# Decay rows of a Mamba-2 mixer picked from transposed cumulated sums by identity columns, and the causal mask moved to VectorE

## The chip, the cores and the metric

The kernel runs on one core of a Trainium2 chip. The metric is the device time of one execution in microseconds (us), as the median of several runs. Below, TensorE is PE in the profile's rows (its weight loads are PEld), VectorE is DVE, ScalarE is ACT, GpSimd is POOL, and SP is the engine that issues the DMAs.

## The reference

Two layers, each a mixer stage and a stage of experts, on 256 tokens of width 1024. The mixer has three groups of heads side by side: windowed attention (6 heads), a bidirectional Mamba-2 (6 heads, 2 chunks of 128 tokens), and differential attention (4 heads). What the change touches is the decay matrix of the Mamba-2 heads:

```python
da = jnp.cumsum((dt * a).reshape(b, nc, SSD_CHUNK, h), axis=2)
lower = jnp.tril(jnp.ones((SSD_CHUNK, SSD_CHUNK), dtype=bool))[None, None, :, :, None]
seg = da[:, :, :, None, :] - da[:, :, None, :, :]
decay = jnp.exp(jnp.where(lower, seg, -jnp.inf))
y_diag = jnp.einsum('bclsh,bcshp->bclhp', jnp.einsum('bclhn,bcshn->bclsh', ch, bh) * decay, xdt)
...
y = y_fwd + y_bwd + d_skip[:, None] * xs
```

For each of 6 heads and 2 directions an exponential is taken of (cumulated sum of the column's token minus that of the row's token), with a mask, and multiplied by the products of C and B.

## The kernel before

**The order.** All engines walk one list, `ORDER`, of named steps (`sc.3`, `row.2.1`); each engine executes those of its own set (`ON_PE`, `ON_DVE`, `ON_ACT`) strictly in the list's order and counts its finished steps in one semaphore. A step on two engines is done by TensorE first, then ScalarE, then VectorE. The list holds for each of the two layers; after it come the 32 experts of the layer, which TensorE works through while SP streams their weights through a ring of 8 slots of 2 MB, each refilled when the step that last reads it is done.

**Steps around the change.** `cum` multiplies `dta` (dt times a, tokens on partitions) by triangles of ones, so that the cumulated sums of all heads lie as columns, tokens on partitions. `cb` makes the C-B products, `xdt` the scaled inputs. `sc.u` are attention scores (TensorE), mask, bias and maximum (VectorE), exponential (ScalarE); `nm.h` normalises them (VectorE); `pT`, `oa`, `od` turn and use them. `vz`, `ck`, `cv` are projections.

**The decay of head h, direction d (`row.h.d`).** TensorE spreads one column of `dta` over 128 columns and multiplies it by a triangle (L583), which gives the cumulated sums as a row that is the same on all partitions; this for three blocks of 128 tokens. For two of them it adds the mask by a bf16 product of `identb` and `smask` (L586). So a step is 3 f32 and 2 bf16 matmuls. ScalarE takes three exponentials from PSUM with the negated column of `cum` as bias into `E[d]` (L834 to L836). VectorE multiplies `E[d]` by the C-B products (L1093 to L1097). `y.h` then does six matmuls with both `E` (L594). There is one `E` for each direction, so the exponentials of head h wait for `y.(h-1)`.

**Banks.** PSUM has 8 banks of 512 f32. A step's bank is given out in turn; `HELD` names the step whose reader must be done before a bank is written again.

Of the kernel before, what the change touches and what calls it, by code (L numbers as in the profile page):

```python
# [132 lines left out]
PE_STEPS = list(COUNT["pe"])  # L133
FIRST_OUT = PE_STEPS.index(("outA", 0))
BANK, HELD = {}, {}
_last, _n = {}, 0
for _i, _s in enumerate(PE_STEPS):
    if _s[0] == "seed":
        continue
    if _s[0] in ("outA", "outB"):  # L140
        BANK[_s] = _s[1]
    elif _s[0] == "ov":
        BANK[_s] = 7
    else:
        BANK[_s] = _n % 8 if _i < FIRST_OUT else 4 + _n % 4
        _n += 1
    if BANK[_s] in _last and _s[0] != "outB":
        HELD[_s] = _last[BANK[_s]]
    _last[BANK[_s]] = _s
# [8 lines left out]
def build_encoder(nc, x_in, cols, rows, w_in, w_out, w_router, w_gate, w_up, w_down, final_w, out):
    with ExitStack() as ctx:
# [583 lines left out]
        def _(act):  # L743
# [16 lines left out]
            for li in range(DEPTH):  # L760
# [3 lines left out]
                for s in STEPS:  # L764
# [58 lines left out]
                    elif kind == "zs":  # L823
                        act.wait_ge(done["dve"], nth(li, "dve", ("silu", 4))) if s[1] == 0 else act.wait_ge(done["dve"], nth(li, "dve", ("zs", 0)))
                        last = A(tmp[:, :], vz[:, s[1], A_K:], ACT.Tanh, scale=0.5)
                    elif kind == "row":
# [1 line left out]
                        c = d * S_H + h
                        act.wait_ge(done["dve"], nth(li, "dve", ("cum",)))
                        if h == 0 and d == 0:  # L830
                            act.wait_ge(done["pe"], nth(li, "pe", ("xs", 1)))
# [503 lines left out]
```

## Time and profile before

| what | value |
|---|---|
| median of 3 runs | 1340.1 us (1339.53 to 1346.42) |
| profiled execution | 1351.05 us, of which 1349.3 us span |
| TensorE busy | 1016.5 us (75%) |
| VectorE busy | 382.1 us (28%) |
| ScalarE busy | 191.6 us (14%) |
| mixer stage of layer 0, of layer 1 | about 12 to 192 us, about 692 to 870 us of the span |

How to read it: a row of the timeline is start, duration, engine, source line, operation, output<-inputs, shapes, and how many records were merged (an f32 matmul leaves two records); in brackets stands how long the engine sat idle before it and what released it. PE's busy time is an upper measure, since its ends are modelled.

### The profile page before, as it was taken

The numbers are of one execution on the slowest core, as the hardware profiler recorded it, in microseconds if no ns is written. First come the engines' busy times: TensorE is split into PE (matmuls) and PEld (weight loads), VectorE is DVE, ScalarE is ACT, GpSimd is POOL, SyncE is SP. The second block draws the span as 40 slices with busy tenths as digits, with TensorE's granted clock in tenths as the row PEclk, the third lists the DMA queues.
The fourth block names the chain that finished last, engine by engine and source line by source line (L and its number), as shares of the span: only waits on it lengthen the run. The fifth ranks groups of instructions, "written<-read, shape, count | busy, mean of one in ns | idle before, by whom it ended". The sixth has DMA issues, their size and how long they took to land.

```text
span 1349.3 us, 26710 instructions
## 1 busy us (share of the span) xinstructions
PE 1016.5 (75%) x11124; PEld 639.6 (47%) x11124; DVE 382.1 (28%) x1160; ACT 191.6 (14%) x549; POOL 9.1 (1%) x28
## 2 busy tenths in 40 slices
PE   5999977766667887767679999766775767766864
PEld 5877753333334443334358777534432433333432
DVE  4456451211212222111144465512111111111112
ACT  2144210000000111000021443100000000000001
POOL 2000000000000000000000000000000000000000
PEclk9899989878888999977979999779877888888887
DMA  9822129999999989799993220289999999999992
GB/s 324 343 93 84 45 88 367 425 424 424 426 426 424 404 335 426 310 403 414 411 377 125 74 115 33 94 347 425 424 425 425 425 424 424 424 426 426 424 419 115
DMA packets 46015, 437.50 MB, mean 324 GB/s; under 512 B 8064, under 2 KB 10112, under 8 KB 21248
## 3 DMA queue, kind: packets, MB, share of 16 engines
q1 hardware_dynamic: 45824, 434.72, 78.1%
q8 instruction: 149, 2.44, 0.7%
q14 instruction: 42, 0.34, 0.1%
HBM read 433.65 MB, written 1.05 MB: 322 GB/s over the span
## 4 chain that ended last, share of the span: by engine, by line
PE 58%; DMA 22%; issue 13%; DVE 5%; ACT 1%; DVEq 1%; ACTq 0%
DMA ring<-in_w_up 22%; PE ps L465 20%; PE ps L537 7%; PE ps L476 7%; PE ps L485 4%; PE ps L446 4%; PE ps L654 4%; PE ps L549 2%; PE ps L609 2%; PE ps L583 1%; PE ps L594 1%; PE ps L553 1%; PE ps L453 1%; PE ps L616 1%; PE ps L633 1%
## 5 line engine op out<-in xcount | busy, mean ns | idle before, releaser
L465 PE MATMUL ps<-ring,xg 128*32 128x256 f32 x4096 | 337.7, 487 | 240.6 <-issue 173.3
L465 PEld LDWEIGHTS ps<-ring,xg 128*32 128x32 f32 x4096 | 173.2, 138 | 386.5 <-issue 348.7
L943 DVE SCALAR_TENSOR_TENSOR gu<-th,ps 128x128 f32<-128x128 f32 x72 | 20.7, 287 | 704.1 <-ACT th L750 704.1
L476 PE MATMUL ps<-ring,actT 128*32 128x256 f32 x2304 | 139.2, 382 | 15.2 <-issue 12.9
L750 ACT ACTIVATE th<-ps 128x128 f32<-128x128 f32 x72 | 20.0, 277 | 609.5 <-PE ps L465 609.5
L476 PEld LDWEIGHTS ps<-ring,actT 128*32 128x32 f32 x2304 | 69.0, 109 | 76.3 <-issue 20.5
L537 PE MATMUL ps<-hT,ring 128*128 128x256 f32 x416 | 97.6, 395 | 1.3 <-DVE hT L993 1.3
L537 PEld LDWEIGHTS ps<-hT,ring 128*128 128x128 f32 x416 | 81.4, 199 | 13.5 <-ACT aneg L788 2.1
L446 PE MATMUL ps<-xh,Pb 128*32 128x256 f32 x1024 | 81.1, 400 | 2.4 <-issue 2.4
L485 PE MATMUL ps<-ysb,PwT 32*128 32x256 f32 x1024 | 75.5, 404 | 2.5 <-issue 1.5
L485 PEld LDWEIGHTS ps<-ysb,PwT 32*128 32x128 f32 x1024 | 47.3, 186 | 32.5 <-issue 29.0
L654 PE MATMUL ps<-ring,hT 128*128 128x256 f32 x256 | 59.1, 389 | 2.9 <-ACT hT L858 1.6
L754 ACT ACTIVATE ysb<-ps 128x256 f32<-128x256 f32 x64 | 24.5, 383 | 234.7 <-PE ps L476 234.7
L654 PEld LDWEIGHTS ps<-ring,hT 128*128 128x128 f32 x256 | 49.0, 195 | 10.4 <-ACT hT L858 2.0
L446 PEld LDWEIGHTS ps<-xh,Pb 128*32 128x32 f32 x1024 | 39.5, 116 | 28.5 <-issue 9.2
L465 PE MATMUL ps<-ring,xgx 128*32 128x256 f32 x512 | 34.4, 428 | 12.2 <-DMA ring<-in_w_up 8.0
L842 ACT ACTIVATE pbuf<-pbuf,nmx 128x256 f32<-128x256 f32 x56 | 28.0, 500 | 58.8 <-DVE nmx L1123 25.4
L953 DVE STREAM_TRANSPOSE xraw<-ps 128x256 f32<-128x256 f32 x72 | 30.0, 417 | 16.8 <-PE ps L446 16.8
L947 DVE STREAM_TRANSPOSE actT<-actv 128x128 f32<-128x128 f32 x72 | 29.3, 407 | 5.8 <-issue 0.5
L465 PEld LDWEIGHTS ps<-ring,xgx 128*32 128x32 f32 x512 | 18.3, 123 | 26.3 <-issue 13.2
L935 DVE TENSOR_TENSOR Pw<-Pb,W 128x256 f32<-128x256 f32 x64 | 27.2, 425 | 6.6 <-issue 0.8
L955 DVE TENSOR_TENSOR xg<-xraw,fnw 128x256 f32<-128x256 f32 x64 | 27.2, 426 | 5.1 <-issue 0.4
(249 smaller groups left out, 831.5 us busy)
## 6 DMA issues: line engine op xcount, KB each, us to landing
ring<-in_w_gate SPq DMA_DIRECT2D x64, 2048.0 KB, 23.7
ring<-in_w_up SPq DMA_DIRECT2D x64, 2048.0 KB, 25.1
ring<-in_w_down SPq DMA_DIRECT2D x64, 2048.0 KB, 19.3
ring<-in_w_in SPq DMA_DIRECT2D x8, 2048.0 KB, 19.2
ring<-in_w_out SPq DMA_DIRECT2D x4, 2048.0 KB, 19.7
ring<-in_w_in SPq DMA_DIRECT2D x2, 1584.0 KB, 14.6
x<-in_x SPq DMA_DIRECT2D x1, 1024.0 KB, 5.1
out<-fin SPq DMA_DIRECT2D x2, 512.0 KB, 2.7
```

What stands on the lines that cost most here:

```text
L446: last = mm(b_prep[j * SLOTS:(j + 1) * SLOTS, 0:DQ], picks[:, t, :], xh[:, t, j * DQ:(j + 1) * DQ], start=(t == 0), stop=(t == TT - 1))
L465: last = mm(b_gate[j * SLOTS:(j + 1) * SLOTS, 0:2 * GQ], tokens[:, k, :], ring[:, low:high + 1:high - low, o:o + GQ], start=(k == 0), stop ...
L476: last = mm(b_y[j * SLOTS:(j + 1) * SLOTS, 0:DQ], actT[:, c * SLOTS:(c + 1) * SLOTS], ring[:, slot, o:o + DQ], start=(c == 0), stop=(c == ...
L485: last = mm(ps[j][:, t * DQ:(t + 1) * DQ], places_[r, t, :], y[r, :], start=False, stop=False, skip_group_check=True)
L537: last = mm(bank[:, 0:SEQ], lhs, hT[:, k, :], start=(k == 0), stop=(k == KC - 1))
L549: last = mm(bank[:, :], hT[:, k, t * P:(t + 1) * P], w[:, k, :], start=(k == 0), stop=(k == KC - 1))
L654: last = mm(bank[:, t * DQ:(t + 1) * DQ], mixT[:, c, t * P:(t + 1) * P], w_half[c // OUT_ROWS][:, c % OUT_ROWS, j * DQ:(j + 1) * DQ], star ...
L842: last = A(pb[:, t, :], pb[:, t, :], ACT.Exp, bias=nmx[:, 1, u, t:t + 1], scale=A_SCALE if u < A_H else C_SCALE, accum_out=den[:, u, t:t + 1])
L935: return v.tensor_tensor(weighted[:, :, :].rearrange("p t (j s) -> p t j s", j=NQ), picks[:, :, :].unsqueeze(2).broadcast_to(four), W[:, : ...
L947: v.transpose(actT[:, :].rearrange("p (c s) -> p c s", c=FC), actv[:, :].rearrange("p (q c) -> p c q", c=FC)).then_inc(S["actT_ready"], 1)
L953: v.transpose(xraw[:, :, :], b_prep[:, 0:DQ].rearrange("p (q k) -> p k q", k=KC))
L955: v.tensor_tensor(to[:, :, :], xraw[:, :, :], fnw[:, :].unsqueeze(2).broadcast_to([P, KC, SLOTS]), ALU.mult).then_inc(S["xg_ready"], 1)
```

## The change

`row` loses its matmuls. In their place:

- `cumT` (once a layer, right after `cum`): 4 matmuls with `dta` as the stationary operand give the cumulated sums transposed, heads on partitions (44 wide: the 12 columns stand twice, at partition 0 and at 32), for 2 directions by 256 tokens. ScalarE copies them to SBUF (`cumT`, in the memory of `yc`).
- `rows.i` (3 a layer, one for heads 2i and 2i+1): 4 matmuls of 12 partitions and 256 columns; the stationary operand is one column of the identity, spread over 128 columns, and picks one row of `cumT` onto all partitions. Direction 0 works from partitions 0 to 11, direction 1 from 32 to 43; each direction has a bank of its own.
- `seg.h.d` (12 a layer, VectorE): two operations of 128x128 add the negated column of `cum` to the row in PSUM and take the minimum with `smask`, which now holds a huge positive number or a huge negative one, into `E[d]`. It waits for `y.(h-1)`, as ScalarE did.
- ScalarE's part of `row` is one exponential of 128x128 from PSUM and one of 128x256 in place in `E[d]`, instead of three.
- The list is changed: `y.0` stands ahead of head 1's decay, `sc.2` ahead of head 2's, `y.4` ahead of `ck.0` and of head 5's.
- Banks are given out by who will be read first, and one step may be held by two.
- `dta` is widened to 44 columns, zeroed in `par` and written by two operations; `identb` goes, `smask` becomes f32.

```diff
-    conv.3 xbc.4 dt silu.2 conv.4 cq.0 xs.0 cq.1 aq.0 silu.3 dta aq.1 xs.1 lam silu.4 aq.2 cum ak cb.0 xdt cb.1 sc.0
-    nm.0 row.0.0 row.0.1 sc.1 vz.0 nm.1 row.1.0 y.0 pT.0 row.1.1 row.2.0 row.2.1 sc.2 y.1 row.3.0 row.3.1 zs.0 sc.3
-    pT.1 y.2 nm.2 vz.1 nm.3 y.3 row.4.0 row.4.1 sc.4 row.5.0 zs.1 row.5.1 ck.0 y.4 ck.1 nm.4 sc.5 pT.2 y.5 pT.3 sc.6
+    conv.3 xbc.4 dt silu.2 conv.4 cq.0 xs.0 cq.1 aq.0 silu.3 dta aq.1 xs.1 lam silu.4 aq.2 cum cumT ak cb.0 xdt cb.1 sc.0
+    nm.0 rows.0 seg.0.0 seg.0.1 row.0.0 row.0.1 sc.1 vz.0 nm.1 y.0 pT.0 seg.1.0 seg.1.1 row.1.0 row.1.1 rows.1 sc.2 y.1 seg.2.0 seg.2.1 row.2.0 row.2.1 seg.3.0 seg.3.1 row.3.0 row.3.1 zs.0 sc.3
+    pT.1 y.2 nm.2 vz.1 nm.3 y.3 rows.2 seg.4.0 seg.4.1 row.4.0 row.4.1 sc.4 y.4 zs.1 seg.5.0 seg.5.1 row.5.0 row.5.1 ck.0 ck.1 nm.4 sc.5 pT.2 y.5 pT.3 sc.6
...
+            _b = min(range(0 if _i < FIRST_OUT else 4, 8), key=lambda k: (read_at(_held_by[k]) if k in _held_by else -1, k))
...
-                    elif kind == "row":
-
-                        _, h, d = s
-                        tri = (upto, since)[d]
-                        c = d * S_H + h
-                        pe.wait_ge(done["dve"], nth(li, "dve", ("cum",)))
-                        for o, t, masked in ((0, 0, True), (1, 1 - d, False), (2, 1, True)):
-                            last = mm(bank[:, o * P:(o + 1) * P], dta[:, t, c:c + 1].broadcast_to([P, P]), tri[:, :],
-                                      start=True, stop=not masked)
-                            if masked:
-                                last = mm(bank[:, o * P:(o + 1) * P], identb[:, :], smask[:, d, :], start=False, stop=True)
+                    elif kind == "cumT":
+
+                        for d, tri in enumerate((upto, since)):
+                            for t in range(TT):
+                                last = mm(bank[0:ROWS, d * SEQ + t * P:d * SEQ + (t + 1) * P], dta[:, t, :], tri[:, :],
+                                          start=True, stop=True)
+                    elif kind == "rows":
+
+                        if s[1] == 0:
+                            pe.wait_ge(done["act"], nth(li, "act", ("cumT",)))
+                        for a in range(2):
+                            for d in range(2):
+                                r = slice(32 * d, 32 * d + 2 * S_H)
+                                c = 32 * d + d * S_H + 2 * s[1] + a
+                                last = mm(ps[BANK["row", 2 * s[1] + 1, d]][:, a * SEQ:(a + 1) * SEQ],
+                                          ident[r, c:c + 1].broadcast_to([2 * S_H, P]), cumT[r, d, :], start=True, stop=True)
...
-                        if h > 0:
-                            act.wait_ge(done["pe"], nth(li, "pe", ("y", h - 1)))
-                        A(E[d][:, 0, :], bank[:, 0:P], ACT.Exp, bias=cum[:, 0, 0, c:c + 1])
-                        A(E[d][:, 1, :], bank[:, P:2 * P], ACT.Exp, bias=cum[:, d, 2, c:c + 1])
-                        last = A(E[d][:, 2, :], bank[:, 2 * P:3 * P], ACT.Exp, bias=cum[:, 1, 0, c:c + 1])
+                        act.wait_ge(done["dve"], nth(li, "dve", ("seg", h, d)))
+                        seg_rows, off = ps[BANK["row", h | 1, d]], h % 2 * SEQ + (1 - d) * P
+                        A(E[d][:, 1, :], seg_rows[:, off:off + P], ACT.Exp, bias=cum[:, d, 2, d * S_H + h:d * S_H + h + 1])
+                        last = A(E[d][:, 0:3:2, :], E[d][:, 0:3:2, :], ACT.Exp)
...
+                    elif kind == "seg":
+
+                        _, h, d = s
+                        dve.wait_ge(done["pe"], nth(li, "pe", ("rows", h // 2)))
+                        if (h, d) == (0, 0):
+                            dve.wait_ge(done["pe"], nth(li, "pe", ("xs", 1), ("cb", 1)))
+                        if h > 0:
+                            dve.wait_ge(done["pe"], nth(li, "pe", ("y", h - 1)))
+                        seg_rows, c = ps[BANK["row", h | 1, d]], d * S_H + h
+                        for t in range(TT):
+                            o = h % 2 * SEQ + t * P
+                            last = v.scalar_tensor_tensor(E[d][:, 2 * t, :], seg_rows[:, o:o + P], cum[:, t, 0, c:c + 1],
+                                                          smask[:, d, :], ALU.add, ALU.min)
```

## Rows read from the trace of the kernel before

**Rows 1.** The page: busy share of the DMA engines in 40 slices, in tenths

```profile
DMA  9822129999999989799993220289999999999992
```

**Rows 2.** Windows: stretch, busy of PE, PEld, DVE, ACT, POOL, granted clock, DMA share, GB/s

```profile
68.00:90.00 22.00, 22.00 (x129) 15.96 (x128) 10.22 (x32) 9.70 (x33) 0.00 (x0) 1.00 0.16 68
...
38.00:42.00 4.00, 4.00 (x13) 3.39 (x14) 2.61 (x8) 0.00 (x0) 0.00 (x0) 0.51 1.02 409
```

**Rows 3.** Timeline of PE, layer 0, from ak to sc.5 and at yT.0

```profile
61.13 3.70 PE L537 MATMUL ps<-hT,ring 128*128 128x256 f32 x16
64.77 1.14 PE L574 MATMUL ps<-xc 64*128 64x256 f32 x8
65.73 1.02 PE L609 MATMUL ps<-akT,aqT 64*128 64x256 f32 x4
...
83.01 1.55 PE L594 MATMUL ps<-xdt,E 128*128 128x64 f32 x12
...
89.11 7.08 PE L549 MATMUL ps<-ring,hT 128*128 128x512 f32 x16
96.03 1.45 PE L594 MATMUL ps<-xdt,E 128*128 128x64 f32 x12
97.31 0.44 PE L583 MATMUL ps<-upto,dta 128*128 128x128 f32 x2
...
99.18 1.13 PE L609 MATMUL ps<-akT,aqT 64*128 64x256 f32 x4
...
106.86 3.67 PE L537 MATMUL ps<-hT,ring 128*128 128x256 f32 x16
110.46 1.13 PE L609 MATMUL ps<-akT,aqT 64*128 64x256 f32 x4
...
126.12 0.55 PE L638 MATMUL ps<-ident,yb 128*128 128x128 f32 x3
```

**Rows 4.** Timeline of DVE, layer 0

```profile
66.79 0.75 DVE L1117 SCALAR_TENSOR_TENSOR pbuf<-distw,ps 128x256 f32<-128x256 f32 x2 [2.89 <-PE ps L609]
...
94.24 0.75 DVE L1117 SCALAR_TENSOR_TENSOR pbuf<-distw,ps 128x256 f32<-128x256 f32 x2 [0.16 <-issue]
...
96.16 0.35 DVE L1101 SCALAR_TENSOR_TENSOR yb<-xtok,rowp,ps 128x128 f32<-128x128 f32 x1
96.60 0.16 DVE L1133 TENSOR_TENSOR den<-den,nmx 128x2 f32<-128x2 f32 x1
...
97.79 0.16 DVE L1133 TENSOR_TENSOR den<-den,nmx 128x2 f32<-128x2 f32 x1
...
100.97 0.29 DVE L1096 TENSOR_TENSOR E<-E,CBs 128x128 f32<-128x128 f32 x1 [0.41 <-ACT E L836]
101.18 0.42 DVE L1097 TENSOR_TENSOR E<-E,CBs 128x256 f32<-128x256 f32 x1
```

**Rows 5.** Timeline of ACT, layer 0

```profile
96.15 0.51 ACT L842 ACTIVATE pbuf<-pbuf,nmx 128x256 f32<-128x256 f32 x1 [2.85 <-DVE nmx L1123]
...
97.51 0.60 ACT L855 ACTIVATE ptb<-ps 128x512 f32<-128x512 f32 x1
...
98.94 0.37 ACT L834 ACTIVATE E<-ps,cum 128x128 f32<-128x128 f32 x1 [0.16 <-DVE pbuf L1138]
99.21 0.36 ACT L835 ACTIVATE E<-ps,cum 128x128 f32<-128x128 f32 x1
...
125.85 0.60 ACT L822 ACTIVATE cv<-ps 128x512 f32<-128x512 f32 x1
```

**Rows 6.** The page, costliest groups: line engine op, shapes, count | busy, mean ns | idle before

```profile
L943 DVE SCALAR_TENSOR_TENSOR gu<-th,ps 128x128 f32<-128x128 f32 x72 | 20.7, 287 | 704.1 <-ACT th L750 704.1
```

**Rows 7.** Timeline of PE, layer 0: `cq.0` (L537) behind `dt`, and `outA.0` (L654)

```profile
38.89 6.68 PE L537 MATMUL ps<-hT,ring 128*128 128x256 f32 x16
...
133.21 7.11 PE L654 MATMUL ps<-ring,hT 128*128 128x256 f32 x24 [0.78 <-ACT hT L858]
```

**Rows 8.** Timeline of PE, layer 1: `outA.0`

```profile
810.53 5.42 PE L654 MATMUL ps<-ring,hT 128*128 128x256 f32 x24 [0.78 <-ACT hT L858]
```

More of the change, by code:

```diff
@@ L74 @@
 NCOL = K_CB + CC
+ROWS = 32 + 2 * S_H
 R_SN = 0
@@ L100 @@
 STEPS = [(name, *map(int, index)) for name, *index in (step.split(".") for step in ORDER.split())]
-ON_PE = {"xT", "xbc", "dt", "cq", "aq", "ak", "cum", "xs", "cb", "row", "sc", "y", "vz", "pT", "ck", "cv", "oa", "od",
+ON_PE = {"xT", "xbc", "dt", "cq", "aq", "ak", "cum", "xs", "cb", "cumT", "rows", "sc", "y", "vz", "pT", "ck", "cv", "oa", "od",
          "yT", "cT", "outA", "outB", "fT", "lg", "seed", "rank", "ov"}
-ON_DVE = {"xc2", "hot", "sq", "xn", "par", "lam", "dt", "dta", "conv", "silu", "cum", "xdt", "row", "sc", "nm", "y", "zs", "ybn", "ycn", "sq2",
+ON_DVE = {"xc2", "hot", "sq", "xn", "par", "lam", "dt", "dta", "conv", "silu", "cum", "xdt", "seg", "row", "sc", "nm", "y", "zs", "ybn", "ycn", "sq2",
           "xn2", "lg", "route", "rank", "ov"}
-ON_ACT = {"sq", "xn", "par", "lam", "dta", "silu", "row", "sc", "vz", "zs", "pT", "ck", "cv", "oa", "od", "yT", "cT", "cq",
+ON_ACT = {"sq", "xn", "par", "lam", "dta", "cumT", "silu", "row", "sc", "vz", "zs", "pT", "ck", "cv", "oa", "od", "yT", "cT", "cq",
           "aq", "ak", "xs", "cb", "sq2", "xn2", "route"}
@@ L129 @@
 FREED_BY = [("xbc", 3), ("cq", 1), ("ak",), ("vz", 1), ("cv",), ("outA", NQ - 1), ("outB", NQ - 1)]
[L133 to L149, printed above, removed]
 def reader(step):
@@ L155, in reader, with tenants, read_at @@
     return "dve" if step[0] in ("dt", "cum", "sc", "y", "lg", "rank", "ov") else "act"
+PE_STEPS = list(COUNT["pe"])
+FIRST_OUT = PE_STEPS.index(("outA", 0))
+AT = {step: i for i, step in enumerate(STEPS)}
+def tenants(step):
+    if step[0] == "rows":
+        return [("row", 2 * step[1] + 1, d) for d in range(2)]
+    return [step]
+def read_at(tenant):
+    at = AT[tenant]
+    if tenant[0] == "pT" and tenant[1] >= 2:
+        h = tenant[1]
+        at = max(at, AT["oa", min(h // 2 - 1, 2)] if h < A_H + 2 else AT["od", h - A_H - 2])
+    return at
+BANK, HELD = {}, {}
+_held_by = {}
+for _i, _s in enumerate(PE_STEPS):
+    if _s[0] == "seed":
+        continue
+    for _t in tenants(_s):
+        if _s[0] in ("outA", "outB"):
+            _b = _s[1]
+        elif _s[0] == "ov":
+            _b = 7
+        else:
+            _b = min(range(0 if _i < FIRST_OUT else 4, 8), key=lambda k: (read_at(_held_by[k]) if k in _held_by else -1, k))
+        BANK[_t] = _b
+        if _b in _held_by and _s[0] != "outB":
+            HELD.setdefault(_s, []).append(_held_by[_b])
+        _held_by[_b] = _t
 def build_encoder(nc, x_in, cols, rows, w_in, w_out, w_router, w_gate, w_up, w_down, final_w, out):
@@ L211, in build_encoder @@
         yc = sb("yc", [P, TT, C_H * C_V], at=q)
+        cumT = yc
         q = [m[0]]
@@ L223, in build_encoder @@
         dts = sb("dts", [P, TT, 2 * S_H], at=m)
-        dta = sb("dta", [P, TT, 2 * S_H], at=m)
+        dta = sb("dta", [P, TT, ROWS], at=m)
         sp = sb("sp", [P, 4, TT * 2 * S_H], at=m)
@@ L502, in _ @@
                     bank = ps[BANK[s]] if s in BANK else None
-                    if s in HELD:
-                        held = HELD[s]
+                    for held in HELD.get(s, ()):
                         pe.wait_ge(done[reader(held)], nth(li, reader(held), held))
@@ L561, in _ @@
                             mm(bank[:, o:o + S_H], upto[:, :], dta[:, t, 0:S_H], start=True, stop=True)
-                            mm(bank[:, o + S_H:o + 2 * S_H], since[:, :], dta[:, t, S_H:], start=True, stop=True)
-                            last = mm(bank[:, o + 2 * S_H:o + 4 * S_H], ones[:, :], dta[:, t, :], start=True, stop=True)
+                            mm(bank[:, o + S_H:o + 2 * S_H], since[:, :], dta[:, t, S_H:2 * S_H], start=True, stop=True)
+                            last = mm(bank[:, o + 2 * S_H:o + 4 * S_H], ones[:, :], dta[:, t, 0:2 * S_H], start=True, stop=True)
                     elif kind == "xs":
@@ L825, in _ @@
                         last = A(tmp[:, :], vz[:, s[1], A_K:], ACT.Tanh, scale=0.5)
+                    elif kind == "cumT":
+                        last = A(cumT[0:ROWS, :, :].rearrange("p d t -> p (d t)"), bank[0:ROWS, :], ACT.Copy)
                     elif kind == "row":
                         _, h, d = s
[L828 to L831, printed above, removed]
[L832 to L836 removed]
+                        act.wait_ge(done["dve"], nth(li, "dve", ("seg", h, d)))
+                        seg_rows, off = ps[BANK["row", h | 1, d]], h % 2 * SEQ + (1 - d) * P
+                        A(E[d][:, 1, :], seg_rows[:, off:off + P], ACT.Exp, bias=cum[:, d, 2, d * S_H + h:d * S_H + h + 1])
+                        last = A(E[d][:, 0:3:2, :], E[d][:, 0:3:2, :], ACT.Exp)
                     elif kind == "sc":
@@ L1000, in _ @@
                         v.tensor_scalar(nsink[:, :], rowp[:, R_SK:R_SK + A_H], -1.0, None, ALU.mult)
+                        v.memset(dta[:, :, :], 0.0)
                         v.memset(xpad[:, :, 0:TAPS // 2], 0.0)
@@ L1065, in _ @@
                         dve.drain()
-                        last = v.tensor_tensor(dta[:, :, :], dts[:, :, :],
-                                               aneg[:, :].unsqueeze(1).broadcast_to([P, TT, n]), ALU.mult)
+                        for o in (0, ROWS - n):
+                            last = v.tensor_tensor(dta[:, :, o:o + n], dts[:, :, :],
+                                                   aneg[:, :].unsqueeze(1).broadcast_to([P, TT, n]), ALU.mult)
                     elif kind == "cum":
```

9 lines of the change are left out of this document (3 added, 6 removed).

## The prediction

> **What bounds the kernel now.** I read the page first, its slices of DMA share. The reader is to see two plateaus of 9 with a low stretch ahead of each [rows 1]: the experts' weights stream at the DMA engines' limit, and the low stretches are the mixers. At a mixer's end the ring is full, so the stream goes on only when the first expert has freed a slot; what a mixer gains or loses is then passed on one to one. The experts' plateau doesn't contain the change.
>
> Then the windows of layer 0's mixer. Where the decay is made, TensorE is busy 22.0 of 22.0 us at full clock, VectorE 10.2 and ScalarE 9.7 [rows 2]. So TensorE is the bound there, and its removed work counts at first sight in full. But VectorE and ScalarE alternate, each waiting for the other, so their half-full columns don't show their slack. For that I read the timelines of the engines side by side [rows 3 to 5]; layer 1 repeats layer 0 shifted by some 677 us, and all working is in layer 0's times, then doubled.
>
> **TensorE's part by itself.** Removed: 12 `row` steps a layer. Two of them run from 97.31 to 99.18 [rows 3], 1.87 us, so six pairs are 11.2 us. Added: `cumT`, 4 f32 matmuls. The six f32 matmuls of `y.3` take 96.03 to 97.31, 0.21 us each, and the change's have twice the columns of these but the same weight loads or smaller; a `row` step's three f32 matmuls bound one at 0.31 (0.93 / 3). I take 0.22, half of what one of 256 columns needs (`ak`: 8 in 3.64 us, 0.45 each); together 0.9, at most 1.2. And three `rows`, each 4 matmuls of 256 columns in two row groups. Their nearest row is `cb`: four such matmuls in two halves of the array, 64.77 to 65.73, 0.96 us, against some 1.06 for the two of an `sc` step that lie in one half (99.18, busy 1.13 for x4 against 1.14 for x8) [rows 3]. I take 0.96; one after the other they would be 2.1. Sum: -11.2 + 0.9 + 2.9 = -7.4 us a layer, -14.9 for both. If nothing else moved, 1340.1 would become 1325.
>
> **What the change adds to the other two engines.** A head's decay is now a chain VectorE, ScalarE, VectorE. Its pieces:
> - `seg` of one direction: two 128x128 operations with a PSUM input. One is 0.287 us in the expert's gate [rows 6] and 0.35 in `y` [rows 4]; a second follows 0.21 later (100.97 to 101.18). I take 0.50, at most 0.56.
> - ScalarE, one direction: the exponential from PSUM to the next, 0.27 (98.94 to 99.21), then one of 256 elements. A 128-element one is 0.37, the 256-element one with a running sum 0.51 [rows 5]. I take 0.42, the bounds are 0.37 and 0.51. So 0.69, and 0.16 between steps.
> - The product, 0.63 (100.97 to 101.60), and 0.10 at each change of engine: after `sc` on VectorE, ScalarE starts at 96.15 where VectorE itself starts its next step at 96.16, so a hand-over costs no more than the boundary of a step.
>
> A head from its first `seg` to its `y`: 0.50 + 0.10 + 0.69 + 0.16 + 0.69 + 0.10 + 0.63 + 0.10 = 2.97 us, with the bounds 2.8 and 3.3. The second direction's `seg` and the first direction's product lie under ScalarE's work. Call this R.
>
> The others, with their gaps: `sc` on VectorE 1.92 (94.24 to 96.16), `sc` on ScalarE 1.36 (96.15 to 97.51), `nm` 1.19 (96.60 to 97.79), `y` on VectorE 0.44.
>
> **Replay of the list.** `cumT` lies on saturated TensorE, so `sc.0` on VectorE starts at 66.79 + 0.9 = 67.69. ScalarE's copy of it (at most the 0.60 of a 512-wide copy, ACT idle there) is hidden: `rows.0` comes three steps later. From there VectorE's queue is one unbroken chain:
> - `sc.0` 1.92, ScalarE 1.36, `nm.0` 1.19, R 2.97: 75.13. Then `sc.1` 1.92, ScalarE 1.36, `nm.1` 1.19, `y.0` 0.44, R 2.97: `y.1` can start at 83.01. Before it started at 83.01 [rows 3]. TensorE goes from 66.63 through `sc.0` 0.96, `rows.0` 0.96, `sc.1` 1.06, `vz.0` 6.92, `y.0` 1.28, `pT.0` about 0.5, `rows.1` 0.96 and `sc.2` 1.06 to 80.3, and stands 2.7 us.
> - `sc.2` is now queued ahead of head 2's `seg` on VectorE and of its exponentials on ScalarE: 1.92 + 1.36, then the rest of R without `seg` (2.97 - 0.60 = 2.37): `y.2` at 88.66. TensorE is free at 85.9 and stands 2.8 us. `vz.1` follows at 89.94, where it started at 89.11.
> - `vz.1` 6.92, `y.3` 1.28, `rows.2` 0.96, 0.2 until its results are there: 99.3. VectorE is through `nm.3` and `y.3` about 0.4 earlier, so `rows.2` is what `seg.4` waits for. R: `y.4` at 102.27; TensorE stood 2.1 us. The move of `y.4` ahead of `ck.0` is what exposes this wait: before, `ck.0` covered it.
> - `y.4` 1.28, `ck.0` and `ck.1` 3.60 each: `sc.5` at 110.75, against 110.46. Head 5's chain (VectorE: `sc.4`, `y.4`, `zs.1`, R) ends about 109.8, hidden under `ck`.
>
> So the 7.4 us saved by TensorE come back as 7.6 us of waiting: +0.3 us a layer, +0.6 in all. Behind this the steps are the same; `yT.0` now takes the bank of `cv`, whose copy ends at 126.45, while it was issued at 126.12 [rows 5, 3]; but `outA.0` waits for ScalarE's copy of `oa.2` [rows 7], and ScalarE works without a pause up to it, so I cost this at nothing (0.4 a layer if that cover is gone). The extra write of `dta`, the zeroing and GpSimd's masks cost nothing, being under the projections; 0.2 us each if they weren't. SP's queue is not moved past anything.
>
> The Trainium skill (TensorEngine Tiling, PSUM Bottleneck) says that tiles speed up TensorE but not the reading of PSUM, which may become the bottleneck. By the TensorE rows alone the sum is -14.9 us; by that page it would be near nothing, as in the replay. No row of the kernel before can show it, since there TensorE doesn't wait in this stretch.
>
> **The clock.** A second price hangs on those waits. TensorE was granted 1.2 GHz (0.51 of full) in 38 to 42 us, right behind the matmuls of 12 columns, and the 8 matmuls there took 6.68 us against 3.70 for the same form [rows 2, 3, 7]: 3.0 lost. `outA.0`, behind two short waits, took 7.11 in layer 0 and 5.42 in layer 1 with the same waits [rows 7, 8]: 1.7 lost once out of twice. A fall costs 2.4 us on average. The new waits of 2.7 and 2.8 us stand ahead of `vz.1`, and the one of 2.1 ahead of `ck.0`, in both layers: four places, each on the path. I count one more fall than before, +2.4.
>
> The forecast is 1340.1 + 0.6 + 2.4 = 1343 us. The rows are of an execution of 1351.05 us (span 1349.3); the sum of differences is applied to the median, 11 us lower, since what sets the two apart lies mostly in the experts and the clock.
>
> **The rivals.**
> - *The clock falls in all four places.* Long `vz.1` and `ck.0` at half clock. For it: both quiet places of layer 0 that I read fell, and the new stretches are quieter. Against it: layer 1's `outA.0` didn't fall. 1340.1 + 0.6 + 9.6 = 1350 us. It decides from three falls on (7.2 + 0.6 is over 0.5%). The Trainium skill (TensorE: Matmul & The Clock Gate, HAM oscillation) describes such losses from gaps between bursts of matmuls.
> - *TensorE stays the bound.* R would have to be some 2 us, or VectorE to be ahead by more than I see. Against it: every piece of R has a row. Then half or all of the 14.9 us stays: 1325 to 1333 us.
> - *`rows` are not side by side.* 2.1 instead of 0.96; only `rows.2` is on the path, 1.15 a layer: 1345 us. Against it: the `cb` row.
>
> **How the numbers follow.** Measurement can't tell 0.5%, 6.7 us, from no change. Forecast 0.50, clock 0.28, TensorE's bound 0.14, serial `rows` 0.08. The forecast's own range is 1339 to 1347: R's bounds (four R a layer on the path, -0.2 and +0.3 each: -1.6 and +2.4 in all), `cumT` up to +0.6, `yT.0` up to +0.8, the clock between none and two falls. Within 0.5% lie 0.46 of the forecast's 0.50, all of the serial case, 0.03 of the clock's (fewer falls) and 0.01 of TensorE's: 0.58. Slower: 0.25 of the clock's and 0.03 of the forecast's (long R with two falls), 0.28. Faster: the rest, 0.14. The range reaches from 1333, the edge of the gain, to 1352.
>
> **What would show it.** Right: no `row` matmuls; TensorE waits 2 to 3 us ahead of `y.1`, `y.2` and `y.4`, released by VectorE's product; from `sc.0` to `sc.5` on TensorE 44 us as now (65.7 to 110.5, now 66.6 to 110.8); a head's chain 3.0 us; `rows` 0.96. Wrong: `y.1` without a wait, or a stretch of under 41 us (then TensorE was the bound), or a granted clock under 0.8 in `vz.1` in both layers (then the clock rival).

## The result, and the profile after

The changed kernel takes 1371.8 us (median of 4 runs, 1363.9 to 1376.0) against 1343.2 for the kernel before in the same series: ratio 1.0207 [1.0144, 1.0270]. Timed once more in the first series of experiments (`again` below) it took 1365.0 against 1347.7: 1.0133 [1.0073, 1.0194]. It is slower, by 1.3% to 2.1%; the forecast was 1343, the range ended at 1352. The profiled execution took 1363.9 us (span 1362.2), the one of before 1351.1 (span 1349.3): these two are 12.9 apart, less than the medians are. The profile of `again` was taken in an execution of 1479.3 us with a lower granted clock (0.69), so its times aren't compared with the others.

The page: busy time of the engines, then the slices of TensorE's granted clock and of DMA share [rows 1].

```profile
PE 1015.7 (75%) x10996; PEld 643.5 (47%) x10996; DVE 397.6 (29%) x1212; ACT 187.9 (14%) x527; POOL 8.8 (1%) x27
...
PEclk9989978898889998988889789878988898888988
DMA  9912128999999989599993121369999999999993
```

TensorE has less work (10996 records, 11124 before) and is hardly less busy (1015.7 us, 1016.5 before): what was removed came back as slower matmuls. The two low stretches of DMA share are still the mixers.

Windows of layer 0 [rows 2], and the ones around `vz.1` in both layers (columns as there):

```profile
68.00:90.00 22.00, 18.88 (x76) 12.34 (x75) 14.77 (x46) 9.06 (x28) 0.00 (x0) 0.79 0.05 21
...
38.00:42.00 4.00, 4.00 (x22) 3.54 (x23) 2.92 (x9) 0.00 (x0) 0.00 (x0) 1.00 1.03 411
...
87.00:97.00 10.00, 10.00 (x28) 5.07 (x27) 6.94 (x22) 4.21 (x12) 0.00 (x0) 0.79 0.00 0
777.00:786.00 9.00, 9.00 (x20) 4.29 (x20) 6.78 (x22) 3.74 (x11) 0.00 (x0) 0.80 0.00 1
```

TensorE now stands 3.1 of 22 us, and its granted clock is 0.79 where it was 1.00. (In 38 to 42 us it stayed up this time; the group that took 6.68 there [rows 7] takes 3.70 here and 6.30 in the profile of `pad` below, so that fall comes and goes.)

The timeline of TensorE, layer 0 [rows 3], then three rows of layer 1:

```profile
58.11 0.60 PE L599 MATMUL ps<-since,dta 128*44 128x128 f32 x4
58.64 3.72 PE L556 MATMUL ps<-hT,ring 128*128 128x256 f32 x16
62.29 1.14 PE L593 MATMUL ps<-xc 64*128 64x256 f32 x8
63.26 1.02 PE L633 MATMUL ps<-akT,aqT 64*128 64x256 f32 x4
64.21 1.13 PE L609 MATMUL ps<-yc,ident 12*128 12x256 f32 x8
65.28 1.13 PE L633 MATMUL ps<-akT,aqT 64*128 64x256 f32 x4
...
79.63 1.60 PE L618 MATMUL ps<-xdt,E 128*128 128x64 f32 x12 [2.31 <-DVE E L1134]
81.16 2.07 PE L633 MATMUL ps<-akT,aqT 64*128 64x256 f32 x4
83.16 1.11 PE L640 MATMUL ps<-ident,pbuf 128*128 128x128 f32 x4
85.08 2.79 PE L618 MATMUL ps<-xdt,E 128*128 128x64 f32 x12 [0.81 <-DVE E L1134]
87.67 8.83 PE L568 MATMUL ps<-ring,hT 128*128 128x512 f32 x16
...
101.86 2.80 PE L618 MATMUL ps<-xdt,E 128*128 128x64 f32 x12 [1.96 <-DVE E L1134]
104.45 9.00 PE L556 MATMUL ps<-hT,ring 128*128 128x256 f32 x32
113.38 1.13 PE L633 MATMUL ps<-akT,aqT 64*128 64x256 f32 x4
...
774.97 2.79 PE L618 MATMUL ps<-xdt,E 128*128 128x64 f32 x12 [0.47 <-DVE E L1134]
777.55 8.63 PE L568 MATMUL ps<-ring,hT 128*128 128x512 f32 x16
...
791.55 2.79 PE L618 MATMUL ps<-xdt,E 128*128 128x64 f32 x12 [1.96 <-DVE E L1134]
```

The waits ahead of `y.1` (79.63), `y.2` (85.08) and `y.4` (101.86) stand where the forecast had them, released by VectorE's last product; they are 2.3, 0.8 and 2.0 us where it had 2.7, 2.8 and 2.1. But behind the first one `sc.3` takes 2.07 instead of 1.13, `pT.1` 1.11 instead of 0.6, `y.2` 2.79 instead of 1.45, `vz.1` 8.83 instead of 7.08; behind the second `y.4` takes 2.80 and the two `ck` 9.00 instead of 7.1. From `sc.0` to `sc.5` it is 50.1 us (63.26 to 113.38) where it was 44.7.

VectorE and ScalarE, head 1's chain [rows 4, 5]:

```profile
76.66 0.61 DVE L1118 SCALAR_TENSOR_TENSOR E<-ps,cum,smask 128x128 f32<-128x128 f32 x2 [0.17 <-issue]
...
79.06 0.42 DVE L1134 TENSOR_TENSOR E<-E,CBs 128x256 f32<-128x256 f32 x1
```

```profile
77.30 0.37 ACT L857 ACTIVATE E<-ps,cum 128x128 f32<-128x128 f32 x1 [1.03 <-DVE E L1118]
77.57 0.41 ACT L858 ACTIVATE E<-E 128x256 f32<-128x256 f32 x1
78.07 0.37 ACT L857 ACTIVATE E<-ps,cum 128x128 f32<-128x128 f32 x1
78.34 0.41 ACT L858 ACTIVATE E<-E 128x256 f32<-128x256 f32 x1
```

From the first `seg` (76.66) to `y.1` (79.63) is 2.97 us, the R of the forecast.

### The profile page after: what moved, and what is told of

The parts are those of the page before. It is cut to its first block, busy times and chain, and to the rows that moved or that the text cites. A ratio compares the mean times of both kernels' runs of the same rounds, so it can differ in the third digit from the quotient of the medians.

```text
span 1362.2 us, 26466 instructions
## 1 busy us (share of the span) xinstructions
PE 1015.7 (75%) x10996; PEld 643.5 (47%) x10996; DVE 397.6 (29%) x1212; ACT 187.9 (14%) x527; POOL 8.8 (1%) x27
## 3 DMA queue, kind: packets, MB, share of 16 engines
HBM read 433.65 MB, written 1.05 MB: 319 GB/s over the span
## 4 chain that ended last, share of the span: by engine, by line
PE 56%; DMA 22%; issue 13%; DVE 5%; ACT 2%; DVEq 1%; SPq 1%; ACTq 0%
DMA ring<-in_w_up 22%; PE ps L485 19%; PE ps L556 7%; PE ps L496 7%; PE ps L505 4%; PE ps L466 4%; PE ps L678 3%; PE ps L568 2%; PE ps L618 2%; PE ps L633 1%; PE ps L572 1%; PE ps L695 1%; PE ps L473 1%; SPq L369 1%; PE ps L657 1%
## 5 line engine op out<-in xcount | busy, mean ns | idle before, releaser
L485 PEld LDWEIGHTS ps<-ring,xg 128*32 128x32 f32 x4096 | 181.2, 137 | 380.2 <-issue 342.4
L496 PE MATMUL ps<-ring,actT 128*32 128x256 f32 x2304 | 139.2, 382 | 15.1 <-issue 11.2
L466 PE MATMUL ps<-xh,Pb 128*32 128x256 f32 x1024 | 84.9, 405 | 6.1 <-issue 6.1
L466 PEld LDWEIGHTS ps<-xh,Pb 128*32 128x32 f32 x1024 | 42.8, 118 | 32.7 <-issue 15.2
L678 PEld LDWEIGHTS ps<-ring,hT 128*128 128x128 f32 x256 | 47.8, 190 | 9.3 <-ACT hT L888 1.9
L568 PE MATMUL ps<-ring,hT 128*128 128x512 f32 x64 | 31.7, 653 | 0.0
L618 PE MATMUL ps<-xdt,E 128*128 128x64 f32 x144 | 24.3, 335 | 9.8 <-DVE E L1134 9.8
L618 PEld LDWEIGHTS ps<-xdt,E 128*128 128x128 f32 x144 | 23.4, 249 | 14.0 <-ACT E L858 7.4
```

The source lines that it names most:

```text
L466: last = mm(b_prep[j * SLOTS:(j + 1) * SLOTS, 0:DQ], picks[:, t, :], xh[:, t, j * DQ:(j + 1) * DQ], start=(t == 0), stop=(t == TT - 1))
L485: last = mm(b_gate[j * SLOTS:(j + 1) * SLOTS, 0:2 * GQ], tokens[:, k, :], ring[:, low:high + 1:high - low, o:o + GQ], start=(k == 0), stop ...
L496: last = mm(b_y[j * SLOTS:(j + 1) * SLOTS, 0:DQ], actT[:, c * SLOTS:(c + 1) * SLOTS], ring[:, slot, o:o + DQ], start=(c == 0), stop=(c == ...
L568: last = mm(bank[:, :], hT[:, k, t * P:(t + 1) * P], w[:, k, :], start=(k == 0), stop=(k == KC - 1))
L618: last = mm(bank[:, t * S_P:(t + 1) * S_P], e[:, blk, :], xdt[:, 0 if e is f else 1, src, hs], start=(n == 0), stop=(n == 2))
L678: last = mm(bank[:, t * DQ:(t + 1) * DQ], mixT[:, c, t * P:(t + 1) * P], w_half[c // OUT_ROWS][:, c % OUT_ROWS, j * DQ:(j + 1) * DQ], star ...
```

## Where the time went, by stages

All stages below are read from the starts on TensorE's timeline, one profiled execution of each kernel, in us, layer 0 / layer 1. The stretch that holds the change, `sc.0` to `sc.6`: before 48.1 / 48.1, after 53.5 / 54.1, together +11.4. On to the first `fT`: 60.2 / 58.5 and 58.5 / 58.9. From the first matmul of layer 0's experts to layer 1's first transposition: 496.7 and 502.1. So between the two profiles, 12.9 apart, the mixers' stretch gives 11.4 and the experts of layer 0 give 5.4; the other stages together take 3.9 off. (Layer 0's 60.2 before holds a fall of the clock at `outA.0`, 1.7 us, which did not come after the change.) Two theories come out of that: the waits cost clock; and something outside the mixers answers to the change. The profiles by themselves show mostly the first. The timeline of TensorE at the first experts, after (first fence) and before (second):

```profile
200.12 5.46 PE L485 MATMUL ps<-ring,xg 128*32 128x256 f32 x64 [2.95 <-issue]
...
214.41 5.14 PE L485 MATMUL ps<-ring,xg 128*32 128x256 f32 x64 [4.98 <-issue]
...
229.05 3.22 PE L485 MATMUL ps<-ring,xg 128*32 128x256 f32 x28 [5.33 <-issue]
```

```profile
209.82 0.84 PE L465 MATMUL ps<-ring,xg 128*32 128x256 f32 x10 [2.19 <-issue]
...
220.05 1.70 PE L465 MATMUL ps<-ring,xg 128*32 128x256 f32 x25 [2.71 <-issue]
...
231.95 0.42 PE L465 MATMUL ps<-ring,xg 128*32 128x256 f32 x4 [3.54 <-issue]
```

TensorE pauses there for nothing that the profile shows, in code that the change doesn't touch, and after the change the pauses lie elsewhere and are longer. (The experts are written out one by one, each behind a branch over its extra passes, `pe.If`. After the change the pauses stand in front of whole groups, x64, right behind that branch; before it they stand inside the groups.) They belong to the kernel and not to one execution: the profile of `again`, the same kernel, has 3.10, 4.99 and 4.92 us ahead of the same three groups. And they don't end there: over all experts of layer 0 the waits on "issue" ahead of these groups sum to 80.2 us before (24 waits) and 94.8 after (28), while the waits for weights ahead of them go from 30.7 to 19.7, so part of the longer pauses only takes the place of waiting for weights.

## The experiments

Each ratio is to the kernel before in the same series, with its 95% interval; the kernel before had medians of 1347.7, 1346.6 and 1346.0 us in the three series.

**First series.**

`again`: the changed kernel as it is. 1365.0 us, 1.0133 [1.0073, 1.0194].

> The changed kernel once more, as the measure for its neighbours. Both theories: some 1.02 times the kernel before (1.014 to 1.027). In its profile TensorE waits about 2.3, 0.5 to 2.7 and 2.0 us ahead of y.1, y.2 and y.4 in both layers, and vz.1 takes 8.6 to 8.8 us instead of 7.1.

`fill`: the three waits are filled with fifteen matmuls whose products nothing reads.

```diff
                     elif kind == "y":
                         h = s[1]
+                        for k in range({1: 5, 2: 6, 4: 4}.get(h, 0)):
+                            mm(bank[:, SEQ:2 * SEQ], ident[:, :], hT[:, k, :], start=True, stop=True)
```

> Idle matmuls of 256 columns (5, 6 and 4, some 0.45 us each) stand ahead of the waits of y.1, y.2 and y.4. If the loss comes from TensorE's clock falling behind the waits (theory A), vz.1 and the ck pair take 7.1 us again, the stretch from sc.0 to sc.5 is some 45 us instead of 50, and the whole comes down by 10 to 20 us against the changed kernel, near the kernel before. If the loss is the chain of waits itself or lies in the experts (theory B), the time stays within 3 us of the changed kernel's.

1343.9 us, 0.9971 [0.9943, 1.0000]. TensorE's timeline, layer 0:

```profile
77.21 2.43 PE L614 MATMUL ps<-hT,ident 128*128 128x256 f32 x10
79.51 1.55 PE L620 MATMUL ps<-xdt,E 128*128 128x64 f32 x12
...
86.42 7.09 PE L568 MATMUL ps<-ring,hT 128*128 128x512 f32 x16
...
100.16 7.13 PE L556 MATMUL ps<-hT,ring 128*128 128x256 f32 x32
107.22 1.13 PE L635 MATMUL ps<-akT,aqT 64*128 64x256 f32 x4
```

`y.1` starts where the chain lets it (79.51; 79.63 without the filler), the clock stays up, `vz.1` takes 7.09 and both `ck` 7.13. From `sc.0` to `sc.6` it is 47.4 in both layers, 6.1 and 6.7 less than without the filler. More work on TensorE made the kernel faster: the clock theory, and its size in the mixers (12.8 us), are shown by this run. The whole came down by 21 us against `again`. From `sc.0` (63.23) to `sc.5` (107.22) it is 44.0 us, which is the replay of the forecast without any fall.

`y4late`: `y.4` behind `ck.0`, as before the change.

```diff
-... row.4.0 row.4.1 sc.4 y.4 zs.1 seg.5.0 seg.5.1 row.5.0 row.5.1 ck.0 ck.1
+... row.4.0 row.4.1 sc.4 ck.0 y.4 zs.1 seg.5.0 seg.5.1 row.5.0 row.5.1 ck.1
```

> y.4 stands behind ck.0 again, as before the change. Theory A: the third wait (2.0 us) goes and with it the fall of the clock over the ck pair (2 us and 1.3 us in y.4): some 5 us less a layer, 10 in all. Theory B (only the wait counts): 2 us a layer, 4 in all.

1364.2 us, 1.0130 [1.0064, 1.0195]; `sc.0` to `sc.6` 49.1 / 48.4. The third wait and its fall are gone, but the time did not come down by the expected 10 us. The planner of the PSUM banks then gave `sc.10` a bank that `outA.0` takes: a new wait of 3.78 us there, in both layers, with a fall of its own behind it (7.50 us instead of 5.42):

```profile
137.39 7.50 PE L678 MATMUL ps<-ring,hT 128*128 128x256 f32 x24 [3.78 <-DVE nmx L1164]
```

`sc.6` to `fT` grows to 63.9 / 64.4. The run told two things apart badly; `y4bank` below repeats it.

`maskonly`: the kernel before with only the mask moved to VectorE (`seg` ahead of each `row` step, its three matmuls kept; no `cumT`, no `rows`).

```diff
                             last = mm(bank[:, o * P:(o + 1) * P], dta[:, t, c:c + 1].broadcast_to([P, P]), tri[:, :],
-                                      start=True, stop=not masked)
-                            if masked:
-                                last = mm(bank[:, o * P:(o + 1) * P], identb[:, :], smask[:, d, :], start=False, stop=True)
+                                      start=True, stop=True)
```

> The kernel before with only the mask moved to VectorE: three f32 matmuls a row step and no bf16 ones, seg ahead of each row. TensorE saves 12 times 0.22 us a layer, and VectorE's chain is as long as in the changed kernel while TensorE is nearly as full. If the chain is what costs, TensorE waits ahead of y.1 and y.2, under 2 us each, and the time lies between 1.00 and 1.01 of before; if the narrow matmuls of rows (12 partitions) are what brings the clock down, there is no fall here and the time is within 3 us of before.

1356.6 us, 1.0079 [1.0047, 1.0112]; `sc.0` to `sc.6` 55.4 / 55.9.

```profile
84.44 2.79 PE L592 MATMUL ps<-xdt,E 128*128 128x64 f32 x12 [3.60 <-DVE E L1101]
87.03 1.59 PE L583 MATMUL ps<-upto,dta 128*128 128x128 f32 x6
```

The chain through VectorE by itself makes the wait (3.60 us, where I expected under 2) and the fall; the matmuls on 12 partitions aren't needed for it.

**Second series.** The changed kernel has 64 matmul records a layer fewer than before (11124 to 10996 in all; an f32 matmul leaves two). These kernels ask whether the length of the program matters.

`pad`: thirty-two matmuls of one column a layer in the waits; `fillpad`: thirty-two of 128 columns.

```diff
+                        for k in range({1: 12, 2: 12, 4: 8}.get(h, 0)):
+                            mm(bank[0:1, SEQ:SEQ + 1], ident[:, 0:1], ident[:, 0:1], start=True, stop=True)
```

```diff
+                        for k in range({1: 11, 2: 12, 4: 9}.get(h, 0)):
+                            mm(bank[:, SEQ:SEQ + P], ident[:, :], hT[:, k % KC, 0:P], start=True, stop=True)
```

> The changed kernel with 32 matmuls of a single column a layer in the waits of y.1, y.2 and y.4, so that TensorE's program has as many instructions again as before the change, while TensorE does next to nothing in the waits. Theory A (the clock alone): as the changed kernel, within 3 us. Theory C (a part of the loss is the place of the code-loading pauses at the first experts, which the shorter program has moved): the waits on nothing ahead of the first experts shrink and the time comes down by some 6 to 10 us; the mixers still show vz.1 at over 8 us.

> The waits filled with 32 matmuls of 128 columns a layer (11, 12 and 9): the same filling time as in the run fill, and the old instruction count. Theory A: as fill, 0.997 of before. Theory C: some 5 us below fill, 0.99 to 0.995 of before.

`pad`: 1358.5 us, 1.0103 [1.0068, 1.0138]; `sc.0` to `sc.6` 54.5 / 53.4, `vz.1` 8.86: the fall stays with one-column matmuls in the waits. `fillpad`: 1341.5 us, 0.9978 [0.9955, 1.0001]; 47.7 / 47.7. TensorE's timeline in layer 1, `y.2` and `vz.1`, `pad` first:

```profile
768.59 2.82 PE L620 MATMUL ps<-xdt,E 128*128 128x64 f32 x12 [0.16 <-DVE E L1136]
771.20 8.85 PE L568 MATMUL ps<-ring,hT 128*128 128x512 f32 x16
```

```profile
755.19 1.45 PE L620 MATMUL ps<-xdt,E 128*128 128x64 f32 x12
756.48 7.08 PE L568 MATMUL ps<-ring,hT 128*128 128x512 f32 x16
```

The two have as many matmuls a layer in the same three waits (12, 12 and 8 against 11, 12 and 9) and differ in the columns of both operands: 12.5 us of TensorE's time in the mixers, 16.8 us in the ratios. On the length of the program they don't agree: `pad` is 4 us below `again`, half of what was expected if the length mattered (6 to 10), inside the two intervals, and `fillpad` came out as `fill` (0.9978 and 0.9971), not 5 us below it.

`y4bank`: `y4late` with one bank kept free for `outA.0`.

```diff
-            _b = min(range(0 if _i < FIRST_OUT else 4, 8), key=...)
+            _b = min(range(4 if _i >= FIRST_OUT else 1 if _i >= PE_STEPS.index(("sc", 9)) else 0, 8), key=...)
```

> y.4 behind ck.0 again, and bank 0 kept from what is written between sc.9 and outA.0, so that outA.0 doesn't wait for the reader of sc.10. Theory A: the stretch from sc.0 to sc.6 is 48 to 49 us, the one to fT 59, as in the changed kernel; the whole is 8 to 10 us below the changed kernel. If the time stays at the changed kernel's, the mixers are not what costs.

1352.5 us, 1.0060 [1.0022, 1.0098]; `sc.0` to `sc.6` 49.1 / 49.0, `sc.6` to `fT` 60.2 / 60.5. Against the changed kernel the third place is worth 4.4 / 5.1 us a layer: the wait of 2.0 that `ck.0` now covers and the fall behind it. (`sc.6` to `fT` is 1.7 us longer than in the changed kernel in both layers: `outA.0` fell there, 7.11 us for 5.42.)

`reord`: the list anew, so that TensorE has long work where the chain is late, and the bank kept free as in `y4bank`.

```diff
-    nm.0 rows.0 seg.0.0 ... y.0 pT.0 ... rows.1 sc.2 y.1 ... sc.3 pT.1 y.2 nm.2 vz.1 nm.3 y.3 rows.2 ... sc.4 y.4 zs.1 ... ck.0 ck.1 nm.4 sc.5
+    rows.0 seg.0.0 seg.0.1 nm.0 row.0.0 row.0.1 sc.1 vz.0 nm.1 y.0 pT.0 seg.1.0 ... rows.1 sc.2 y.1 seg.2.0 ...
+    zs.0 sc.3 pT.1 nm.2 vz.1 nm.3 y.2 rows.2 seg.3.0 ... sc.4 y.3 seg.4.0 ... ck.0 y.4 zs.1 seg.5.0 ... ck.1 nm.4 sc.5
```

> The changed kernel with another list: seg of head 0 runs under ScalarE's exponential of sc.0, vz.1 stands ahead of y.2, y.4 behind ck.0 and y.5 behind ck.1, so that the long projections cover the decay chains; bank 0 kept free as in the run y4bank. By my replay the waits are near 1 us ahead of y.1 and y.3 and none elsewhere. Theory A: the clock holds, the stretch from sc.0 to sc.6 is 42 to 45 us against 48 before the change, and the time is 1325 to 1338 us, below both. If the list isn't the cause, it stays near the changed kernel.

1356.0 us, 1.0077 [1.0046, 1.0107]; `sc.0` to `sc.6` 49.3 / 47.8. Two waits are left, as short as I expected, but the clock doesn't hold: it falls behind both (a `y` takes 1.45 at full clock):

```profile
81.72 2.45 PE L619 MATMUL ps<-xdt,E 128*128 128x64 f32 x12 [1.00 <-DVE E L1135]
...
99.80 2.79 PE L619 MATMUL ps<-xdt,E 128*128 128x64 f32 x12 [1.40 <-DVE E L1135]
```

**Third series.**

`reordfill`: `reord` with fifteen matmuls of 128 columns in those two waits; `reordfillpad`: with thirty-two of 64 columns.

```diff
+                        for k in range({1: 6, 3: 9}.get(h, 0)):
+                            mm(bank[:, SEQ:SEQ + P], ident[:, :], hT[:, k % KC, 0:P], start=True, stop=True)
```

```diff
+                        for k in range({1: 13, 3: 19}.get(h, 0)):
+                            mm(bank[:, SEQ:SEQ + 64], ident[:, :], hT[:, k % KC, 0:64], start=True, stop=True)
```

> The reordered list (rows.0 ahead of nm.0, vz.1 ahead of y.2, y.4 behind ck.0, y.5 behind ck.1) with fifteen float32 matmuls of 128 columns, six ahead of y.1's wait and nine ahead of y.3's, whose products nothing reads. The clock alone (theory 1): the two waits that were left (1.00 and 1.40 us) are filled, the clock stays up, vz.1 takes 7.1 us and the stretch from sc.0 to sc.6 47.4 to 47.7 us instead of 49.3 and 47.8; the program is 34 matmuls shorter than the kernel before, so if the length matters the pauses at the first experts stay as in the changed kernel: 1350 to 1356 us. Rival (length is nothing): as the filled kernels, 1341 to 1345.

> The same list with thirty-two float32 matmuls of 64 columns (thirteen and nineteen) in the same two waits: the same filled time, but as many matmuls a layer as the kernel before. If the length matters: pauses at the first experts of 1.2 to 3.5 us as in the kernel before, 1340 to 1344 us, and 6 us or more below the fifteen-matmul version. If it doesn't: equal to the fifteen-matmul version within 3 us.

`reordfill`: 1339.3 us (11 runs), 0.9942 [0.9915, 0.9968], the only kernel here whose interval lies below the kernel before. `sc.0` to `sc.6` is 44.1 / 45.8 where before has 48.1: the saving on TensorE that the change was costed at is there, less the filler. The time lies just below the 1341 to 1345 expected if the length of the program is nothing, and far from the 1350 to 1356 if it matters. `reordfillpad`: 1355.5 us, 1.0100 [1.0066, 1.0133]; 54.3 / 52.6. I had expected both to keep the clock, and the second didn't. TensorE's timeline, layer 0, `reordfill` first:

```profile
79.39 1.60 PE L615 MATMUL ps<-hT,ident 128*128 128x128 f32 x12
80.83 1.45 PE L621 MATMUL ps<-xdt,E 128*128 128x64 f32 x12
...
94.12 2.27 PE L615 MATMUL ps<-hT,ident 128*128 128x128 f32 x18
96.23 1.45 PE L621 MATMUL ps<-xdt,E 128*128 128x64 f32 x12
97.52 3.67 PE L557 MATMUL ps<-hT,ring 128*128 128x256 f32 x16
```

```profile
95.68 7.41 PE L615 MATMUL ps<-hT,ident 128*128 128x64 f32 x38
102.88 2.77 PE L621 MATMUL ps<-xdt,E 128*128 128x64 f32 x12
105.44 6.14 PE L557 MATMUL ps<-hT,ring 128*128 128x256 f32 x16
```

The 64-column records take 0.195 us each (7.41 / 38) and no wait stands between them: TensorE is busy 17.0 of 17.0 us in 95 to 112, at a granted clock of 0.60. In layer 1 of `reordfill` the clock fell in the 128-column filler too for a while (3.82 us for the same 18 records), which is most of the 1.7 us between the layers. So this filler isn't safe either; it only falls less often.

`padstart` and `beforepad`: the changed kernel and the kernel before, each with thirty-two one-column matmuls a layer in front of the first transposition, on the path there (1.7 us a layer).

```diff
                             pe.wait_ge(done["dve"], nth(li, "dve", ("xn",)))
+                            for _ in range(32):
+                                mm(bank[0:1, 0:1], ident[:, 0:1], ident[:, 0:1], start=True, stop=True)
```

> The changed kernel with thirty-two one-column matmuls a layer in front of the first transposition, on the path there (1.5 us a layer, 3 us in all), and none in the waits: the loss of clock in the mixers stays whole (sc.0 to sc.6 53.5 to 54.5 us). If the length of the program ahead of the experts matters: their pauses shrink to those of the kernel before and the time is that of the kernel with the same matmuls in the waits plus 3: 1358 to 1364. If only what the waits held mattered: 1368 to 1375.

> The kernel before with the same thirty-two one-column matmuls a layer at the same place, 3 us on the path. If pauses at the experts depend on how the program lies, they change against 2.2, 2.7 and 3.5 us, in either direction, and the time leaves 1.0022 (3 us over the kernel before) by more than 0.3%; if they do not, the ratio is 1.001 to 1.004.

`padstart`: 1361.6 us, 1.0103 [1.0066, 1.0140]; its `sc.0` to `sc.6` is 54.3 / 54.1. Less its own 3.4 us it stands at 1.0078, below the changed kernel's 1.0133 and 1.0207, though nothing was put in the waits; the distance to the first of these lies within the intervals, that to the second doesn't. `beforepad`: 1354.4 us, 1.0059 [1.0029, 1.0089], that is 4.5 us more than its 3.4, with the mixers unchanged (48.1 / 48.1). So the same insertion seems to have taken time off the one kernel and put time on the other. Neither is clear: the second step, 0.34%, is just over its own interval of 0.3%.

All kernels side by side. "Ratio" is that of the series in us ((ratio - 1) x 1346); "mixers" is the difference from before in `sc.0` to the first `fT`, both layers (214.9 before), with the 3.4 of their own path for `padstart` and `beforepad`; "rest" is what is left; "pauses" is the sum of TensorE's "issue" waits over 0.5 us ahead of the experts' first matmuls in 195 to 235 us of the profile.

| kernel | ratio | mixers | rest | pauses |
|---|---|---|---|---|
| changed, two series | +27.9, +17.9 | +10.0 | +17.9, +7.9 | 13.3 |
| y4late | +17.5 | +10.9 | +6.6 | 13.0 |
| reord | +10.4 | +2.9 | +7.5 | 13.1 |
| y4bank | +8.1 | +3.9 | +4.2 | 11.0 |
| beforepad | +7.9 | +3.2 | +4.7 | 11.9 |
| before | 0 | 0 | 0 | 9.0 |
| pad | +13.9 | +10.4 | +3.5 | 5.2 |
| padstart | +13.9 | +14.3 | -0.4 | 5.3 |
| reordfillpad | +13.5 | +11.1 | +2.4 | 7.0 |
| fill | -3.9 | -2.8 | -1.1 | 9.5 |
| fillpad | -3.0 | -0.5 | -2.5 | 7.5 |
| reordfill | -7.8 | -5.9 | -1.9 | 0.7 |
| maskonly | +10.6 | +17.8 | -7.2 | 2.8 |

The five kernels with pauses of 11 to 13 us have a rest of 4 to 18 us, the others one of -7 to +4. With 3 to 9 us of uncertainty on each ratio, and mixers and pauses from one profile each, that is a pattern, not a measurement of one pause. It also rests on the first 40 us of the experts: over all experts of layer 0 the waits on "issue" ahead of these groups are 95.7 us in `fillpad`, as many as in the changed kernel (94.8), and `fillpad` isn't slower. It isn't the count of matmuls: `reordfill` and `fill` are 34 records a layer short of the kernel before and among the best, `beforepad` is 64 over it and among the worse.

## Why the prediction was wrong, point by point

- *TensorE's part* was right within 0.1 a term: `cumT` 1.00 us (57.64 to 58.64; forecast 0.9), each `rows` 1.06 (64.21 to 65.28) instead of 0.96, so side by side, as a `cb`. The rival of serial `rows` is out. That the saving is real shows in `reordfill`: from `sc.0` to `sc.6`, ahead of which `cumT` lies, 48.1 - 11.2 + 3.2 (three `rows`) + 3.9 of filler (1.60 + 2.27) gives 44.0, measured 44.1 in layer 0.
- *R*, 2.97 us, was measured at 2.97, and its pieces lie near their forecasts: 0.64 from the first `seg` to ScalarE (76.66 to 77.30) instead of 0.60, 0.77 between ScalarE's two directions instead of 0.85.
- *The replay* held: `sc.0` to `y.1` 16.38 us forecast, 16.37 measured; with the waits filled `sc.0` to `sc.5` is 44.0 of 44.1 forecast. "+0.3 us a layer" is right when the clock stays up. The Trainium skill (TensorEngine Tiling, PSUM Bottleneck) warns that the reading of PSUM may become the bottleneck when TensorE gets faster. The gain did come to nothing, but the trace shows no full reader of PSUM: VectorE is busy 14.8 of 22 us. It is the chain of two engines in turn.
- *The bank of `yT.0`*: its wait is there, 0.31 us. The stage behind `sc.6` is 0.3 us longer in layer 1 (58.9 for 58.5); in layer 0 it is not, the fall at `outA.0` left aside (58.5 for 60.2 - 1.7). Costing it at nothing held within 0.3 a layer.
- *The clock: the step that failed.* "I count one more fall than before, +2.4." It fell in all four places, in every profile used of a kernel that kept those waits (the changed kernel, `pad`, `padstart`), and each cost 3.2 us and not 2.4: 6.1 and 6.7 a layer by `fill`, two falls each. The 2.4 was a mean over two long matmul groups alone, and the forecast left out the short work between the wait and the long group: `sc.3` +0.9, `pT.1` +0.5, `y.2` +1.3 stand ahead of `vz.1`'s own +1.75. The first two were taken out of the wait ahead of `y.2` (2.8 forecast, 0.81 measured), the others were not. I had counted one because `outA.0` fell once in two layers; but behind its wait wide matmuls come first, and behind these a dozen of 64 columns. (`outA.0` fell in 7 of 24 places, in the profiles of the twelve kernels that keep its two short waits. That what stands behind the wait makes the difference fits `reordfillpad`; it wasn't tried by itself.) With four falls at 3.2 the forecast's own sum gives 1340.1 + 0.6 + 12.8 = 1353.5 us. That is 10 us above the forecast, where the measured differences from before are 29 and 17 us for 3 forecast: the step explains more than half of the miss in the second of these and less than half in the first. The clock rival named the mechanism and all four places; its 1350 was short by the size of the falls (9.6 for 12.8) and by the rest below.
- *What no part of the forecast had*: 8 to 18 us outside the mixers (the rest of the table, from the medians; between the two profiled executions all but 3 of the 12.9 us lie in the mixers). "The experts' plateau doesn't contain the change" is true for the code, and perhaps not for the time. The runs point to the program itself, without showing it: one-column matmuls placed elsewhere take about 8 us of this rest away (the changed kernel's lower series against `padstart`) and add 4.7 to the kernel before. That it is the fetching of TensorE's instructions, which come to lie otherwise, is argued and not shown: the pauses have no releaser in the profile, and it wasn't found what decides their length. Open also is why the changed kernel's two series differ by 10 us, which is inside their intervals.

## What to carry over

When a change shortens the bound engine's work but puts a chain of other engines behind it, its waits have to be priced twice: once as time, and once as the slower clock of everything that TensorE issues next, the short matmuls included. Before giving up such a change, reorder the list so that wide matmuls lie where the chain is late; wide matmuls nobody reads in the waits that remain were worth 1.2% to 1.6% here (`fill` against `again`, `fillpad` against `pad`, `reordfill` against `reord`). And differences under 0.5% of a long unrolled program aren't to be read as the edit's own until a version with dummy instructions elsewhere has been timed beside it.

## What the runs showed of the hardware

- Behind a wait of 1.0 us between groups of matmuls the granted clock fell from 2.4 to 1.2 GHz (`reord`: `y.1` 2.45 us instead of 1.45). The Trainium skill (TensorE: Matmul & The Clock Gate, A second HAM failure mode: psum-queue depth-cycling) tells of small idles between groups doing this, and the trace agrees; here it happened in every profile with these waits.
- The clock can fall with no idle time at all: 38 records of 64 columns back to back in `reordfillpad`, TensorE 100% busy, 0.195 us each and a clock of 0.60. (What came ahead of it stood at full clock: 26 such records in 3.12 us, 0.12 each, in the same profile, as fast as records of 128 columns, 2.27 / 18 = 0.126 us.)
- Two f32 pairs of 12-partition matmuls in two row groups ran side by side: 1.07 us for four of 256 columns (64.21 to 65.28), as long as the two of an `sc` step take (1.05, 65.28 to 66.33).
- At the first experts TensorE pauses up to 5.7 us at a time without a releaser (`y4bank`). The place and length of these pauses differ between kernels whose code there is the same, and are nearly the same in two executions of one kernel.
